# Delta scan: lower merging levels in 64x64 parts of the array with a joint Gram product, and the first index tile prepared one stage earlier

## The reference, cut to what matters

```
def hybrid_layer(x, cond, ...):                 # twice
    mod = cond @ w_ada + b_ada
    shift, scale, gate = split(mod, 3)
    h = layer_norm(x) * (1 + scale) + shift
    proj = h @ w_in                             # q_idx, k, val, k_idx, w_idx first
    ...
    return layer_norm(ALPHA * x + gate * y, ln_g, ln_b)

def chunk_gated_delta_rule(q, k, v, g, beta):   # 8 heads, forward and flipped
    g = cumsum(g)                               # inside a chunk
    decay = exp(where(tril, g[:, None] - g[None, :], -inf))
    L = tril(einsum(k_beta, k) * decay, -1)
    T = triangular_solve(eye + L, eye)          # unit lower triangular inverse
    u, w = T @ v_beta, T @ (k_beta * exp(g))
    a_intra = einsum(q, k) * decay
    def step(state, xs):
        v_new = u_c - w_c @ state
        o = (q_c * exp(g_c)) @ state + a_c @ v_new
        state = state * exp(g_last) + k_dec.T @ v_new
```

## Time and profile before

| | us |
|---|---|
| median of 3 runs | 3689.68 (3685.44 to 3692.49) |
| the profiled execution | 3680.2 |
| its span, first to last instruction | 3678.2 |
| busy: PE / weight loads (PEld) | 3138.2 / 2536.9 |
| busy: VectorE (DVE) / ScalarE (ACT) / GpSimd (POOL) | 2146.1 / 1372.8 / 1140.9 |
| mean granted TensorE clock | 0.936 |

### The profile page before, as it was taken

The page is one execution under the profiler, slowest core; times in us unless marked ns, Lnnn a source line. Parts: engine busy times, 40 slices in busy tenths (PEclk is TensorE's granted clock), DMA queues, the critical chain, the costliest instruction groups (busy, mean ns, idle before and its releaser), DMA issues. The chain is left out here.

```text
span 3678.2 us, 43621 instructions
## 1 busy us (share of the span) xinstructions
PE 3138.2 (85%) x15729; PEld 2536.9 (69%) x15729; DVE 2146.1 (58%) x4123; ACT 1372.8 (37%) x2729; POOL 1140.9 (31%) x1248
## 2 busy tenths in 40 slices
PE   4899878868998788598998998968878688899788
PEld 3578645645776456487887886768867688688567
DVE  5699787556996876576772005457755577101223
ACT  1366345213763551235662212444323443121221
POOL 1236311221462113422004242225422344423310
PEclk9999999989998999799999999989989799899899
DMA  5322411531223125410002113123231331412511
GB/s 199 123 78 92 131 44 55 172 127 52 78 90 128 44 63 175 150 41 6 1 1 95 49 63 117 31 56 89 48 109 29 73 80 46 158 49 103 174 66 46
DMA packets 233337, 306.24 MB, mean 83 GB/s; under 512 B 40959, under 2 KB 149247, under 8 KB 230945
## 3 DMA queue, kind: packets, MB, share of 16 engines
q1 hardware_dynamic: 221602, 282.47, 24.8%
q10 hardware_dynamic: 11520, 20.98, 1.6%
HBM read 243.48 MB, written 59.90 MB: 82 GB/s over the span
## 5 line engine op out<-in xcount | busy, mean ns | idle before, releaser
L669 PE MATMUL psum<-qs,hT 128*128 128x512 f32 x1344 | 308.7, 391 | 9.5 <-POOL qs L756 9.3
L2342 PE MATMUL psum<-hTs,cws 128*128 128x512 f32 x1152 | 284.3, 408 | 33.2 <-POOL hTs L2589 29.5
L669 PEld LDWEIGHTS psum<-qs,hT 128*128 128x128 f32 x1344 | 252.5, 189 | 65.6 <-POOL qs L756 7.6
L2342 PEld LDWEIGHTS psum<-hTs,cws 128*128 128x128 f32 x1152 | 226.3, 198 | 82.8 <-POOL hTs L2589 30.3
L2093 PE MATMUL psum<-bhsn,bringn 128*128 128x512 f32 x1152 | 264.8, 392 | 14.1 <-POOL bringn L2138 13.3
L2093 PE MATMUL psum<-bhsa,bringa 128*128 128x512 f32 x1152 | 264.1, 392 | 9.4 <-POOL bringa L2138 9.4
L2093 PEld LDWEIGHTS psum<-bhsn,bringn 128*128 128x128 f32 x1152 | 217.7, 189 | 61.1 <-issue 13.6
L2093 PEld LDWEIGHTS psum<-bhsa,bringa 128*128 128x128 f32 x1152 | 218.1, 189 | 55.4 <-issue 9.8
L1403 PE MATMUL psum<-w_out,oys 128*128 128x512 f32 x768 | 180.0, 396 | 27.2 <-DVE w_out L1462 25.6
L1403 PEld LDWEIGHTS psum<-w_out,oys 128*128 128x128 f32 x768 | 146.6, 192 | 61.3 <-DVE w_out L1462 27.2
L836 DVE TENSOR_SCALAR_CACHE_REDUCE junk<-score,cand 128x384 uint8<-128x384 f32 x248 | 186.8, 810 | 2.2
(11 more groups left out here) (449 smaller groups left out, 6998.0 us busy)
## 6 DMA issues: line engine op xcount, KB each, us to landing
stg<-in_w_in SPq DMA_DIRECT2D x96, 256.0 KB, 2.7
wa<-in_w_ada SPq DMA_DIRECT2D x32, 512.0 KB, 3.5
pj<-ptmp ACTq DMA_DIRECT2D x64, 256.0 KB, 2.2
dlb<-blocks SPq DMA_DIRECT2D x32, 512.0 KB
dlb<-in_w_in SPq DMA_DIRECT2D x24, 512.0 KB, 3.9
wa<-in_w_ada SPq DMA_DIRECT2D x8, 1024.0 KB, 8.5
oyf<-yTd SPq DMA_DIRECT2D x16, 512.0 KB, 4.7
ostg<-in_w_out SPq DMA_DIRECT2D x16, 512.0 KB, 6.0
```

The source lines that it names most:

```text
L669: mm = pe.matmul(bank(m), lhs, rhs, start=(kc == 0 and x == 0), stop=(kc == KC - 1 and x == 2))
L2342: mm = pe.matmul(ps[:, u % 4, :], ws[c % 2][:, a, kc, :], hs[:, b, kc, half * HALF:(half + 1) * HALF], start=(kc == 0 and x == 0), stop=(k ...
```

## The change

In the scan, X, T and a new Td hold only the two 64 wide diagonal blocks of each head (64 columns instead of 128), with the block's row in the partitions. `left` and `right` of the two lower levels become, for each head, four products in 64x64 parts: both r and both blocks b. `left` and `right` take both r in one go and wait for both first. The Gram products of k and q are one product with 256 moving columns from a joint tile `qkT`. ScalarE copies the merged blocks to TT (`spread`), whose other quarters GpSimd clears once in each scan.

The first tile of each layer's index inputs gets a class of its own, `FirstTile`: its x, its statistics, its turn and modulation, and the loads of `w_qi` and `w_sm` go into `stage_conditioning` for layer 0 and into `stage_first_output` of layer 0 for layer 1. The semaphores are recycled before each `stage_first_output` and once behind the second layer.

```diff
@@ class FirstTile (new)
+    def load_x(self, sp, x_in):
+        sp.dma_start(self.x[:, :], x_in[0:P, :]).then_inc(self.s_x, 16)
+    def load_w(self, sp):
+        w = self.k.t["w_in"][self.l].rearrange("(k p) n -> p k n", p=P)
+        sp.dma_start(self.w_qi[:, :, :], w[:, :, QI0:KI0]).then_inc(self.s_w, 16)
+        sp.dma_start(self.w_sm[:, :, 0:2 * HD], w[:, :, K0:ZB0]).then_inc(self.s_w, 16)
+        sp.dma_start(self.w_sm[:, :, 2 * HD:], w[:, :, KI0:D_IN]).then_inc(self.s_w, 16)
+    def stats(self, dve):
+        dve.wait_ge(self.s_x, 16)
+        for i in range(2):
+            dve.bn_stats(self.st[:, i, :], self.x[:, i * HALF:(i + 1) * HALF]).then_inc(self.s_st, 1)
+        dve.wait_ge(self.s_st, 2)
+        dve.bn_aggr(self.mv[:, :], self.st[:, :, :]).then_inc(self.s_mv, 1)
...
+    def turn(self, pe):
+        pe.wait_ge(self.s_xn, 1)
+        turn_tile(pe, self.k, 0, self.x, KC).then_inc(self.s_xT, 1)
+    def modulate(self, act):
+        k, l = self.k, self.l
+        act.wait_ge(self.s_xT, 1)
+        for kc in range(KC):
+            ins = act.activation(self.hf[:, kc, :], k.ps[:, kc // 4, (kc % 4) * P:(kc % 4 + 1) * P], ACT.Identity,
+                                 bias=k.modcol[:, l, kc:kc + 1], scale=k.modcol[:, l, KC + kc:KC + kc + 1])
+        ins.then_inc(self.s_hf, 1)
@@ stage_conditioning: SP behind the last piece; GpSimd; PE behind the sums; ACT; DVE behind the last piece
+            first.load_x(sp, k.t["x"][0])
+            first.load_w(sp)
+            first.rstd(pool)
+            first.turn(pe)
+            first.modulate(act)
+            first.stats(dve)
+            first.normalise(dve)
@@ stage_first_output: SP; PE behind the last tile; ACT behind the last y_hi; GpSimd; DVE
+                if first and n == 3:
+                    sp.wait_ge(s_st[0], 16)
+                    first.load_x(sp, x_out)
+                    first.load_w(sp)
+            if first:
+                pe.wait_ge(s_g, NT - SLOTS + 1)
+                first.turn(pe)
+            if first:
+                first.modulate(act)
+                if first and n == 5:
+                    first.rstd(pool)
+                if first and n == 6:
+                    first.stats(dve)
+                if first and n == 7:
+                    first.normalise(dve)
@@ stage_delta, PE
+                pe.wait_ge(s_NLT, u)
+                pe.wait_ge(s_AT, u)
+                pairs = ps[:, 2:4, :].rearrange("p b (h x q) -> p (b h) x q", h=HG // 2, x=2)
                 for h in range(HG):
-                    mm = pe.matmul(gbank(0)[:, h, :], d.kT[:, h, tk(st, r)], d.kT[:, h, tk(st, r)], start=True, stop=True)
+                    mm = pe.matmul(pairs[:, h], d.kT[:, h, tk(st, r)], d.qkT[:, :, h, tk(st, r)], start=True, stop=True)
...
+            def left(st, s):
+                for r in range(2):
+                    u = 2 * st + r
+                    if s == 0:
+                        pe.wait_ge(s_turn, u + 1)
+                        if u >= 2:
+                            pe.wait_ge(s_last, u - 1)
+                    else:
+                        pe.wait_ge(s_mg, 4 * st + r + 1)
                 for h in range(HG):
-                    mm = pe.matmul(low(lbank(r), r, s)[:, h], NLT[st % 3][r][:, h, :], low(T[r], r, s)[:, h],
-                                   start=True, stop=True)
-                mm.then_inc(s_Xp, 1)
+                    for r, b in ((0, 0), (1, 1), (0, 1), (1, 0)):
+                        at = slice(W * b, W * (b + 1))
+                        mm = pe.matmul(low(lbank(r), r, s)[at, h], NLT[st % 3][r][at, h, at], low(T[r], r, s)[at, h],
+                                       start=True, stop=True)
+                        if h == HG - 1 and r != b:
+                            mm.then_inc(s_Xp, 1)
...
+                        mm = pe.matmul(high(lbank(r), r, s)[at, h], X[r][at, h, :], high(Td[r], r, s)[at, h],
+                                       start=True, stop=True)
@@ stage_delta, ACT: called for both r behind keep_x of level 1
+            def spread(st, r):
+                act.wait_ge(s_mg, 4 * st + r + 1)
+                if st >= 3:
+                    act.wait_ge(s_P, 2 * (st - 3) + r + 1)
+                else:
+                    act.wait_ge(s_T0, 1)
+                for b in range(2):
+                    at = slice(W * b, W * (b + 1))
+                    act.activation(TT[st % 3][r][at, :, at], Td[r][at, :, :], ACT.Copy).then_inc(s_spread, 1)
             def merge_half(st, r):
                 act.wait_ge(s_mg, 4 * st + 2 + r + 1)
+                act.wait_ge(s_spread, 4 * st + 2 * r + 2)
@@ stage_delta, GpSimd
+            pool.tensor_tensor(near[:, :], k.cst[:, C_B16:C_B16 + W], k.cst[:, C_B16 + W:C_B16 + P], ALU.add).then_inc(s_near, 1)
+            pool.wait_ge(s_near, 1)
...
+                dst = Td[0] if r == 0 else T[1]
+                pool.tensor_tensor(dst[:, :, :].rearrange("p h (b i) -> p h b i", i=16), bc(Tc[:, r, :, :], 2, W // 16),
+                                   bc(near[:, :].rearrange("p (b i) -> p b i", i=16), 1, HG), ALU.mult).then_inc(s_wide, 1)
...
+                if now == TIMES[0]:
+                    for i in range(3):
+                        for r in range(2):
+                            ins = pool.memset(TT[i][r][:, :, :], 0.0)
+                    ins.then_inc(s_T0, 1)
@@ stage_delta, DVE
-                link(dve.copy_predicated(high(TT[st % 3][r], r, 0), high(m, r, 0), high(lbank(r), r, 0)))
-                cs = slice(0, 96) if r == 0 else slice(32, P)
-                dve.transpose(T[r][:, :, cs], TT[st % 3][r][:, :, cs]).then_inc(s_mg, 1)
+                link(dve.copy_predicated(high(Td[r], r, 0), high(m, r, 0), high(lbank(r), r, 0)))
+                dve.transpose(T[r][:, :, :], Td[r][:, :, :]).then_inc(s_mg, 1)
@@ build
-                stage_first_output(k, l, x_in, t["x1"] if l == 0 else t["x2"])
                 k.recycle_semaphores()
+                tile0 = FirstTile(k, early, l + 1) if l + 1 < DEPTH else None
+                stage_first_output(k, l, x_in, t["x1"] if l == 0 else t["x2"], tile0)
+            k.recycle_semaphores()
```

More of the change, by code:

```diff
@@ L225, in stage_conditioning @@
+def stage_conditioning(k, first):
     nc, t, ps = k.nc, k.t, k.ps
@@ L227, in stage_conditioning @@
         acc = k.sb(ctx, "mod_acc", [P, 2 * KC, P])
[L228 removed]
+        wa = [k.sb(ctx, f"wa{i}", [P, 2 * D]) for i in range(4)]
+        cd = Conditioning(k, ((0, 0, 2 * D),), [w[:, :] for w in wa], (acc[:, :, :],))
         c_col = k.sb(ctx, "c_col", [P, KC])
@@ new lines, in right @@
+            def right(st, s):
+                for r in range(2):
+                    pe.wait_ge(s_X, 3 * 2 * st + 2 * s + r + 1)
+                for h in range(HG):
+                    for r, b in ((0, 0), (1, 1), (0, 1), (1, 0)):
+                        at = slice(W * b, W * (b + 1))
+                        mm = pe.matmul(high(lbank(r), r, s)[at, h], X[r][at, h, :], high(Td[r], r, s)[at, h],
+                                       start=True, stop=True)
+                        if h == HG - 1 and r != b:
+                            mm.then_inc(s_Y, 1)
@@ L2962, in _ @@
                 if inv:
-                    left(now, 0, 0)
-                    left(now, 1, 0)
+                    left(now, 0)
                 if scan:
@@ L2969, in _ @@
                 if inv:
-                    right(now, 0, 0)
-                    right(now, 1, 0)
+                    right(now, 0)
                 if prep and now == 0:
@@ L2976, in _ @@
                 if inv:
-                    left(now, 0, 1)
-                    left(now, 1, 1)
+                    left(now, 1)
                 if scan:
@@ L2981, in _ @@
                 if inv:
-                    right(now, 0, 1)
-                    right(now, 1, 1)
+                    right(now, 1)
                 if scan:
@@ L3089, in _ @@
                     keep_x(now, 1, 1)
+                    spread(now, 0)
+                    spread(now, 1)
                 if prep:
```

201 lines of the change are left out of this document (102 added, 99 removed).

## The result

| | before | after | ratio, 95% interval |
|---|---|---|---|
| median, us | 3691.09 (3685.44 to 3700.91, 4 runs) | 3649.64 (3648.47 to 3662.6, 4 runs) | 0.9893 [0.9862, 0.9924] |
| repeated with set 2 | 3693.05 (9 runs) | 3659.42 (3649.82 to 3666.51, 5 runs) | 0.9914 [0.9898, 0.9929] |
| span of the profiled execution | 3678.2 | 3648.3; repeated 3648.0 | |
| mean granted clock | see table before | 0.930; repeated 0.929 | |

A forecast was written before the change was run, and what follows sets the result against it. A scan step's first half hangs on VectorE and GpSimd, not PE. 23 us from the scans plus 17 from the first tiles, 40 off 3689.7, gives 3650 us; range 3628 to 3678.

The forecast's parts named there:

- TensorE's groups: Scan, each `left` or `right` of both directions: 0.93 us plus 0.34 for the mode change, instead of 1.79.
- Rival 3: Scan: 64x64 parts do not overlap, so groups take 2.20 us instead of 1.79; 3699 us in all, chance 0.07.
- The Gram product: Scan: joining eight 128-column products into four of 256 saves nothing; up to 0.9 us if weight loads bound it.
- The gaps: Scan step: PE waits about 2.5 us before the second `left` and 1.7 before the last one.
- `spread`: Scan: four ScalarE copies a step, 0.373 us each, 1.5 in all, covered by ScalarE's 1.97 us idle before `weigh`.
- The scans' 23 us: Both delta scans: twelve inner steps at 1.7 us give 20, four outer at 0.75 give 3; bounds 0 and 50.
- with 2 us less work for PE I count 0.5 back: Inner scan steps: 0.5 us a step regained from stretches at 1.2 GHz, where PE sets the pace.
- Rival 1: Scans: a lower clock eats the gain, leaving 0 to 8 us; 3665 to 3673; 0.30, shared with scans gaining nothing.
- sign of being wrong: Scan: among the signs against the forecast, a mean granted clock under 0.88 in steps 2 to 7.
- From there works without a break to the merge at 2547.49 (8.4 us): Scan step: VectorE, after the second turn ends at 2539.10, works 8.4 us without a break to the merge.
- no wait of its own: Scan: `decayed` now waits for the joint Gram product, but gains no wait, since r=0's Gram is ready well before.
- The first tiles' 17 us: Way into both projection stages: layer 0 gains 7.2 us, layer 1 net 10.1 (14.1 - 3.0 - 1); 17.3 together.

The follow-up runs named there:

- set 2: Second set of follow-up runs on one chip, the only one timing the changed kernel again beside the kernel before: 3659.42 against 3693.05 us.
- scan_only: The kernel before with only the edits inside the delta scan, first tiles left as they were: 3666.28 us, ratio 0.9936.
- tiles_only: The kernel before with only the early first tiles, their weight loads and the moved recyclings, scan left as it was: 3675.82 us, ratio 0.9966.
- after_again: The changed kernel timed and profiled once more, nothing edited: 3659.42 us, ratio 0.9914 to the kernel before.
- before_fill: The kernel before with four useless 128-column products in TensorE's gap ahead of the second merging's first product: 3682.15 us, ratio 0.9976.
- turn_twice: The changed kernel with VectorE's first transpose of each half of a scan step done twice: 3665.04 us, ratio 0.9930 to the kernel before.
- fill_one: The changed kernel with eight useless 128-column products ahead of each step's second `left`, from the second step on: 3646.75 us, ratio 0.9891 to the kernel before.
- fill_half: The changed kernel with four useless 128-column products ahead of each step's second `left`: 3642.27 us, ratio 0.9866 to the kernel before.

## Why the prediction was right, and where it wasn't

- **The number**: 3650 forecast, 3649.64 measured, and 3659.42 in the repetition. That the first agrees to half a us is luck; the sizes of the two parts, 23.6 and 12.5 us for 23 and 17, and the whole of 40 and 32 for 40, are what bears the forecast out.
- **TensorE's groups** (0.93 + 0.34 us, with full overlap of the parts): right. A group of 32 and leaving the mode take 1.06 us, for 0.93 + 0.15. Rival 3, no overlap, is out by the same row. The Gram product: right at nothing saved. The gaps, 2.5 forecast before the second `left` and 1.7 before the last: 2.19 and 1.78 us. `spread`: 0.41 us a copy and not 0.37, under cover as said.
- **The scans' 23 us**: timed at 23.6 (16 to 31) in scan_only. In the profiles both scan stages together go from 498.8 and 504.8 us (before, tiles_only) to 486.3, 478.9 and 490.8 (after, after_again, scan_only), 16.5 less on average. One term is right: at full clock most steps take 26.1 or 26.2 us in before and before_fill and 24.9 in most filled new ones, locked, so 1.2 to 1.3 less, for 1.2 forecast. The other is not: "with 2 us less work for PE I count 0.5 back" for the clock. The clock in the inner steps fell, from 0.92 to 0.88, 0.90 and 0.87 in the profiles of after, after_again and scan_only, and nothing came back. Rival 1 had that mechanism right, and the prediction's own sign of being wrong, a clock under 0.88 in these steps, was met in scan_only. Of the 1.7 us that an inner step was to save, these profiles show 0.86, 1.74 and 0.57; the one that reaches it does so by steps of 22.3 to 23.9 us out of the contention, which the forecast didn't know. So that the scans' number came near 23 is in part luck.
- **"From there works without a break to the merge at 2547.49 (8.4 us)"**: taken as a fixed length, and it isn't. 3.5 us of it was VectorE waiting for GpSimd inside four instructions (4.61 against 1.12 us). That is the step of the reading that failed. From the end of the substitution to the second `left` are 12.83 us before; the forecast's terms (1.07 less, 0.37 more) give 12.1; after, it is 12.32 in locked steps and 11.0 to 11.3 in the repeated run's steps out of the contention. It did not cost the prediction its number, but it hid that the same work can take 27.4, 26.2 or 23.8 us a step. Nor did the joint Gram product gain "no wait of its own": once the four are short, VectorE waits 0.63 us for it in the step of 23.8 us shown above, and 2.86 in turn_twice.
- **The first tiles' 17 us**: 12.5 measured (8 to 18). The hand-overs were right: layer 0's first projection came 8.0 us earlier (7.2 forecast), layer 1's 12.8 on top of the 8.6 that layer 0's output stage had in hand (13.1 forecast: the 14.1 less the 1 charged; the moved and the added recycling lie outside), and tile 7 was held up by the 1 us charged. What was mis-sized lies behind them: part of the gain is gone by the end of the stage, and the later groups depend on the granted clock. The same 16 products of tile 1 in the profile after and in fill_one, whose code up to there is the same:

```profile
60.38 7.13 PE L474 MATMUL psum<-w_qi,score 128*128 128x512 f32 x16 [2.99 <-ACT score L510]
```

```profile
61.81 8.58 PE L474 MATMUL psum<-w_qi,score 128*128 128x512 f32 x16 [3.00 <-ACT score L510]
```

  Of the eleven profiles with the new tiles, layer 0's index stage ended at 169.6 to 170.2 us in four and at 173.6 to 175.6 in seven, against 177.4 to 178.4 in the three with the old: 5.0 us gained on average (7.2 forecast). From layer 0's output stage to the end of layer 1's index stage are 232.5 us on average against 243.0: 10.4 gained, of the same 13.1.
- **Not foreseen**: the attention input stage takes 196.9 to 198.1 us in every profile of a kernel with the new tiles and 195.0 to 195.3 in the others, though its code is the same. The largest difference between the traces of before and after is one wait for a weight that GpSimd splits; first before, then after:

```profile
1545.74 9.24 PE L1653 MATMUL psum<-fw,fhs 128*128 128x512 f32 x39 [1.62 <-POOL fw L1606]
```

```profile
1525.42 11.54 PE L1727 MATMUL psum<-fw,fhs 128*128 128x512 f32 x42 [3.37 <-POOL fw L1680]
```

  What makes GpSimd late there is open. Two more stretches grew, the ones that hold the moved and the added recycling, by 2.1 and 0.8 us, close to the 3.0 charged. At the start of dense attention, behind all of this, the eleven profiles stand at 1681.2 us on average and the three others at 1692.2: 11.0 us for the first tiles, beside the 12.5 timed.
- **What stays open**: fill_half was the fastest kernel, 17 us under the changed one. Whether GpSimd's row products can be put where VectorE's substitution doesn't meet them, and what that gives without a doubled transpose, was not tried. A filled locked step of 24.9 us is about 1 us above one of 23.8 out of the contention; unfilled, 27.4 and 23.8 are more than 3 apart.

## What to carry to other kernels

Before an engine's stretch is taken as a fixed length, compare the duration of one instruction in it with its best case in the same trace; 0.28 against 1.27 us was in the trace of before, in plain sight. Taking work off TensorE lengthens its gaps, and here gaps of 2.2 us were followed by half clock each time: a few useless products in the gap brought the clock in the steps from 0.88 to between 0.94 and 1.00, and the kernel was 12 to 17 us faster in the set that timed both. And a saving that a profile of one execution shows or doesn't show (3.2 or 15.3 us for the same scan) needs the timed runs or a second profile beside it.

## What the runs showed of the hardware

- Products on two 64x64 parts overlap fully in the order 0, 1, 1, 0: one every 0.029 us, and 0.13 to 0.16 us to leave the mode. Two row parts of one direction write one PSUM bank in this order without a visible price.
- Two-input VectorE instructions in SBUF, 0.28 us alone, took 1.0 to 1.4 us beside GpSimd's two-input products; the transposes (0.40 to 0.45 over 256 columns) and the two-input ones that read PSUM (0.65 to 0.69) kept their time.
- A group of 16 products took 7.13, 8.58 or 10.20 us in one place at one code, at a granted clock of 1.00, 0.83 and 0.70 in it.
